# Routing ahead of the diagonals in the expert loop of a two-layer hybrid trunk

## The reference, cut to what matters

```python
q = (xt @ w_query).reshape(T, PEER_HEADS, 2, PEER_DHALF)
s = jnp.einsum('thpd,pkd->thpk', q, sub_keys)
s_a, i_a = lax.top_k(s[:, :, 0], 16)
s_b, i_b = lax.top_k(s[:, :, 1], 16)
cand_s = s_a[..., :, None] + s_b[..., None, :]        # 16 x 16 candidates
cand_i = i_a[..., :, None] * 128 + i_b[..., None, :]
top_s, pos = lax.top_k(cand_s, 16)
idx  = take_along_axis(cand_i, pos)
gate = softmax(top_s)
u = u_tab[idx]
act = gelu(einsum('thkd,td->thk', u, x))
out = einsum('thk,thkd->td', gate * act, v_tab[idx])
```

## Time and profile before

| what | value |
|---|---|
| median of three runs | 2417.72 us (2416.97 to 2420.75) |
| the profiled execution | 2420.75 us, its span 2419.0 us |
| PE busy | 2023.2 us, 84% of the span |
| DVE busy | 1678.4 us, 69% |
| POOL busy | 987.3 us, 41% |
| ACT busy | 366.2 us, 15% |
| mean granted clock of PE | 0.922 of full |
| read from HBM | 713.35 MB |

### The profile page before, as it was taken

How to read it: one execution, slowest core, us unless ns; L and a number is a source line. 1 busy time by engine, 2 the same in 40 slices (tenths; PEclk the granted TensorE clock), 3 DMA queues, 4 the chain that set the end, 5 groups by cost and what they waited for, 6 DMA issues and landing times.

```text
span 2419.0 us, 21962 instructions
## 1 busy us (share of the span) xinstructions
PE 2023.2 (84%) x6485; PEld 1195.3 (49%) x6485; DVE 1678.4 (69%) x4247; ACT 366.2 (15%) x828; POOL 987.3 (41%) x909
## 2 busy tenths in 40 slices
PE   6999999966888788888869999997588787878876
PEld 5776676643334334333337777675344333434432
DVE  3266776766777777778743677867577867777785
ACT  0222222201010101101002222221110101111010
POOL 2355565523434434343403354333234343443432
PEclk8999998977999999999989999998899999998989
DMA  9856555427999999999995456732499999999996
GB/s 313 218 139 171 159 163 154 138 69 305 418 417 407 420 402 418 416 403 419 404 322 142 131 145 168 199 132 63 182 417 418 421 408 415 411 416 406 413 409 258
DMA packets 331567, 715.49 MB, mean 296 GB/s; under 512 B 12475, under 2 KB 262611, under 8 KB 265811
## 3 DMA queue, kind: packets, MB, share of 16 engines
q0 software_dynamic: 73728, 536.90, 53.9%
q1 hardware_dynamic: 257750, 177.54, 26.0%
HBM read 713.35 MB, written 1.05 MB: 295 GB/s over the span
## 4 chain that ended last, share of the span: by engine, by line
PE 40%; DVE 26%; DMA 18%; issue 9%; POOL 4%; ACT 1%; SPq 1%; DVEq 0%; POOLq 0%
DMA wall<-in_peer_uv,idx 18%; PE PS L909 15%; PE PS L737 7%; PE PS L732 6%; DVE wall L951 3%; PE PS L800 3%; POOL wall L545 3%; DVE wall L948 2%; PE PS L742 2%; PE PS L888 2%; DVE ring L1146 2%; DVE M L945 1%; DVE pos L1260 1%; DVE ts L1257 1%; DVE M L1300 1%
## 5 line engine op out<-in xcount | busy, mean ns | idle before, releaser
L909 PE MATMUL PS<-wall,M 128*128 128x512 f32 x2048 | 989.8, 637 | 272.6 <-DVE M L945 272.3
L545 POOL DMA_INDIRECT wall<-in_peer_uv,idx x512 | 559.1, 1092 | 783.4 <-PE PS L909 460.6
L909 PEld LDWEIGHTS PS<-wall,M 128*128 128x128 f32 x2048 | 404.2, 203 | 832.5 <-issue 454.2
L951 DVE CUSTOM_DVE_ANT_0 wall<-wall,tok 128x1024 f32<-128x1024 f32 x512 | 607.1, 1223 | 299.2 <-DMA wall<-in_peer_uv,idx 295.4
L732 PE MATMUL PS<-hT,wall 128*128 128x256 f32 x1280 | 286.6, 384 | 6.0 <-DMA wall<-in_w_in 5.2
L732 PEld LDWEIGHTS PS<-hT,wall 128*128 128x128 f32 x1280 | 244.6, 192 | 41.8 <-issue 6.8
L737 PE MATMUL PS<-wall,hT 128*128 128x512 f32 x512 | 228.0, 599 | 0.0
L667 ACT ACTIVATE dg<-dg 128x2 f32<-128x2 f32 x256 | 52.3, 204 | 1098.0 <-DVE dg L951 1098.0
L492 POOL TENSOR_TENSOR braw<-braw,cact 128x1024 f32<-128x1024 f32 x80 | 154.2, 1928 | 75.7 <-DMA braw<-in_ada_w 75.7
L474 POOL TENSOR_SCALAR rsb<-ms 128x4 f32<-128x4 f32 (+2 forms) x23 | 4.5, 194 | 404.3 <-DVE ms L951 404.3
L945 DVE TENSOR_SCALAR M<-ident,dg,gate 128x128 f32<-128x128 f32 x512 | 153.9, 344 | 0.0
(11 more groups left out here) (219 smaller groups left out, 1992.1 us busy)
## 6 DMA issues: line engine op xcount, KB each, us to landing
wall<-in_w_in SPq DMA_DIRECT2D x128, 704.0 KB, 8.6
braw<-in_ada_w SPq DMA_DIRECT2D x80, 512.0 KB, 3.6
ring<-in_peer_w_query SPq DMA_DIRECT2D x14, 1024.0 KB
wall<-in_w_out SPq DMA_DIRECT2D x2, 4096.0 KB, 17.6
wall<-in_peer_uv,idx POOLq DMA_INDIRECT x512
wall<-in_ada_w SPq DMA_DIRECT2D x6, 1024.0 KB, 10.8
ring<-in_ada_w SPq DMA_DIRECT2D x2, 1024.0 KB
pwt<-in_pool_w SPq DMA_DIRECT2D x8, 256.0 KB, 3.6
```

What stands on the lines that cost most here:

```text
L545: nc.gpsimd.indirect_dma_start(out=pair_rows[b][s], out_offset=None, in_=uv_rows, in_offset=bass.IndirectOffsetOnAxis(ap=idx[t][:, k:k + 1 ...
L909: i = mm(bank(B_ACC + 2 * t + hf), diag[:, b, s, :], pair_rows[b][s][:, D + hf * 512:D + (hf + 1) * 512], start=False, stop=(g // HGROUPS ...
L951: return v.tensor_tensor_reduce(out=o, in0=a, in1=b, scale=1.0, scalar=0.0, op0=ALU.mult, op1=ALU.add, accum_out=acc)
```

## The change

`diag_group(g)` moves from before the routing piece of its step to after it. Nothing else is changed; the same instructions are issued.

```diff
                     if g + 1 < LGROUPS:
                         dot_group(g + 1)
-                    diag_group(g)
                     nh, nt = (h, 1) if t == 0 else (h + 1, 0)
                     if nh < HEADS:
                         if q == 0:
...
                             route_pairs(nh, nt)
                             route_end(nh, nt, False)
                             ch.sync()
+                    diag_group(g)
```

## The result

The changed kernel takes 2456.48 us (median of 4 runs, 2448.78 to 2467.47) against 2419.23 us for the kernel before (4 runs, 2416.97 to 2421.50). The ratio is 1.0157, 95% interval 1.0113 to 1.0202: slower by 1.6%, 38 us. The profiled execution took 2460.79 us. The forecast was 2430 with a range of 2412 to 2455, so its direction held and its size didn't.

A forecast was written before the change was run, and what follows sets the result against it. The prediction took full DMA transfers in the expert phases as the bound, with little ring slack after routing. Fourteen tiles with queries at 0.9 us added 12.6 us, all else 0, to 2417.72: 2430 us, range 2412 to 2455.

The forecast's parts named there:

- What bounds the kernel now: Expert phases: DMA transfers are full (share 1.01, 413 GB/s), engines have room; the six-buffer ring has little slack after routing.
- q = 0 and 1 cost nothing: First two of a tile's eight groups: diagonals and expert sums come 1.8 us later, covered by early gathers; cost 0.
- The delay of PE and of the issues: At q = 2 PE starts 6.9 us later; next tile's gathers issue 6.4 us (q = 0) and 4.6 us (q = 1, 2) later.
- The floor of the flight: A gather with nothing queued ahead takes 9.36 us from first issue to dot products, against 12.95 us in the chain.
- The step that failed: Tiles with queries (t = 0, heads 0 to 6): 0.9 us each, bounds 0 and 2.2; 14 tiles give 12.6 us.
- t = 1 tiles cost 0, bounds 0 to 11 us: Tiles without queries: cost 0, at most 0.7 us each, over 14 tiles and the last head's two t = 0 tiles.
- Hidden altogether: Rival for the whole kernel: transfers are the bound and the delay only eats waiting time; 2418 us, chance 0.33.
- the chain of waits is literal: Rival: flights stay at 12.95 us, so each of 14 tiles grows by 4.6 us; 64 us, 2482 us, chance 0.14.
- Faster: Rival: PE's slow restart moves from q = 3 to q = 2 and, if cheap, tiles shorten; 2397 us, chance 0.07.

The follow-up runs named there:

- the cut load: Kernel before the change, with 128 KB of the next head's query weights loaded in place of 1 MB: 0.9877; the same cut in the changed kernel: 1.0116.
- the earlier gathers that brought nothing: Kernel before the change, with both halves of PE's queries moved after the sum of q = 1: 0.9988, 2417.38 us.
- the half delay: Kernel before the change, with the diagonals of q = 2 inside the routing, behind the top 16 of the sums: 1.0004 to the kernel before, 2421.72 us.
- the longer one: Changed kernel with the diagonals of q = 2 still later, behind the dot products of q = 4: 1.0428 to the kernel before, 2526.64 us.

## Why the prediction was wrong, point by point

- *What bounds the kernel now* held. Transfers bound the tiles (the cut load, and the earlier gathers that brought nothing), with little slack at the head of a tile.
- *q = 0 and 1 cost nothing* held: 1.0007.
- *The delay of PE and of the issues* held. New issue times forecast for the tile were 16.8, 23.7 and 30.6 us from its q = 3; the means are 16.22, 23.14 and 30.09. PE's slow sum was taken at 6.02 us; in the tile shown it is 5.64.
- *The floor of the flight* held. I took 9.36 us from the lone gather at the start of the phase; q = 0, 1 and 2 took 9.66, 9.45 and 10.27 us on the mean. With it the forecast put the arrivals of q = 0 to 2 at 26.2, 33.1 and 40.0 (776.2, 783.1 and 790.0 less 750.03); they are 25.88, 32.59 and 40.36. By the rule of the Trainium skill that the prediction weighed ("DMA: Bandwidth & Descriptors", section "Anatomy of one DMA — SWDGE (gpsimd) path"), a flight would be 6.8 us, an estimate, and nothing would be late. The trace does not agree: counted from the issue of a group's first gather to its dot products, no mean flight of the kernels before and after is under 9.4 us, and the measurement decides.
- *The step that failed* is the last one of that part: "so I stay nearer the middle than the upper end: 0.9 us". The tile's own sum gave 1.3 us for q = 3 and I went below it. Measured is 2.61 us, above even the upper bound of 2.2. Three things make up the difference.

  First, I took 0.4 us off the sum's own 1.3, on the ground that the query load moves into the gaps. But SP issues that load only when the queries are done, and these are late by the same PE delay. In the tile shown that is at 698.96 us, well into the second of the two thin windows:

```profile
698.96 0.40 SPq L341 DMA_DIRECT2D ring<-in_peer_w_query  x1
```

  Second, the tile that I worked with was a slow one: its period was 43.57 us (793.60 less 750.03) where the mean of the 14 was 42.83. Against the mean, the same new times give 0.74 us more. I had even noted that in some tiles PE kept its clock and "the sums become later by 1.7 us more", and then left that out of the sum. The issues of q = 1 and 2 came 5.3 us later on the mean, where I had 4.6.

  Third, the arrival of q = 3 was forecast 44.9 us from the reference point and came at 45.44. The forecast had no query load in it; the two tiles without one came at 44.93, the 12 with one at 45.52, since the load lengthens the flight of q = 2. So the load belonged in the sum as a cost of about 0.6 us and not as a relief of 0.4. Nor does each tile with queries fetch it, as the prediction says, but 12 of the 14.

  0.4, 0.74 and 0.57 (45.44 less 44.87) are 1.71, which with 0.9 is the 2.61 measured.
- *t = 1 tiles cost 0, bounds 0 to 11 us*: in the changed kernel the period of the tiles without queries is the same (40.77 against 40.84). Late diagonals in the t = 1 tiles alone cost 0.3% (7 us), inside the bounds.
- *Hidden altogether* is refuted, as is *the chain of waits is literal*: the issues of q = 2 came 5.3 us later and the tile grew by 2.6. Of the rest 2.0 us came off the flight, 12.3 to 10.3 us, and 0.7 off the distance from q = 2 to q = 3 (5.74 us before, 5.08 after). The threshold of the loss shows in the half delay (no cost) and its slope in the longer one (2.4 for 2.5 us). The chain is literal once the flights have reached their floor, and only then. *Faster* is refuted too.
- The sum: 12.6 us were forecast, 14 times 2.61 is 36.5, and 38 were measured by the ratio (37.3 by the medians, 2456.48 less 2419.23).

Why PE's restart takes longer when only the t = 1 diagonals are late was not settled, nor where the 2 of the 7 us lie that the periods of those tiles don't explain.

## What to carry to other kernels

In this ring of buffers a delay cost max(0, delay less slack), and the slack was the flight today less the flight of a lone transfer. Both can be read from a trace, from issue to use: here 12.3 us, and 9.5 us at the floor. Take the mean over all tiles and not one tile, and count which releases go late together: a filler load that waits for the same engine fills the gap that this engine's delay opens only in part (0.6 us of its 2.3 were still paid for here). If an engine must wait, put its independent work (here PE's queries) under the wait and not behind it: that gave back three quarters of the loss. Where nothing was lost, in the kernel before, it brought 0.1% at best.

## What the runs showed of the hardware beyond that

The restart at the low clock is short but sits in a bad place: after 5.64 us of idling, with the granted clock at 0.50 (1.2 GHz), the sum of q = 2 took 5.64 us where one takes 3.45. An estimate from these rows: without the 2.2 us between them the issue of q = 2 would be 3.1 us late in place of 5.3, and 0.3 us over the slack of 2.8. No run here takes the restart away and leaves the queries where they are. With PE's queries under the routing, four sums took 13.90 us in the tile shown, 3.5 each. The changed kernel also spreads more from run to run: 2448.78 to 2467.47 against 2416.97 to 2421.50.
